# Masked copy of the transposed probabilities moved from VectorE to GpSimd, and the order of the attention units on TensorE

## The chip, the cores and the metric

The kernel runs on one core of a Trainium2 chip. The metric is device time in microseconds (us), the median of three runs. All times below are microseconds unless marked ns.

## What is computed

One decoder layer over 1024 tokens of width 1024. One input projection feeds two token mixers: a gated linear recurrence with four heads, and a sliding-window attention with eight query heads, two key/value heads of 64 columns, a window of 128 and a learned sink for each head. Their outputs go through one output projection into the residual stream, and a gated feed-forward layer follows. The attention part of the reference, cut to what matters:

```python
qb = q.reshape(B, nb, BLOCK, ATTN_KV_HEADS, ATTN_GROUP, ATTN_HD)     # blocks of 128 queries, 256 keys: previous, current
scores = jnp.einsum('bnqhgd,bnkhd->bnhgqk', qb, kb)
mask = (rel >= 0) & (rel < WINDOW) & (kpos >= 0)
scores = jnp.where(mask, scores, NEG_INF)
m = jnp.maximum(jnp.max(scores, axis=-1, keepdims=True), s)
p = jnp.exp(scores - m)
denom = jnp.sum(p, axis=-1, keepdims=True) + jnp.exp(s - m)
out = jnp.einsum('bnhgqk,bnkhd->bnqhgd', p / denom, vb)
```

## The kernel before, in words

Each engine is programmed by its own block, and the blocks for TensorE (PE), VectorE (DVE), ScalarE (ACT), GpSimd (POOL) and SyncE (SP) all walk through one list, `order`, that `schedule()` writes. An engine does the steps that concern it in the order of that list and waits on semaphores for the others. Nothing is reordered at run time, so the place of a step in the list is its place in the queue of every engine that takes part in it.

Attention stands in the list as 16 units (2 for each of the 8 blocks of 128 tokens; a unit i is four heads of block i // 2). Since a window of 128 over blocks of 128 means that each query sees exactly 128 keys, the scores of the previous and the current block are merged into one 128 x 128 square for each head (`sc`, three buffers). The steps of a unit:

- `SC`: PE computes the scores (12 matmuls on 64-row tiles of the array, L1511 to L1515); DVE copies the previous block's scores (L1871), lays the current block's over them by a predicate (L1874) and takes the row maximum (L1880). The next unit's `SC` on PE waits for L1874.
- `SE`: ACT takes the exponentials, four instructions with their sums (L1009).
- `SN`: DVE takes the reciprocal of the sums (L1885); POOL multiplies the probabilities by it (L759) and writes a small sink column (L706).
- `TR`: PE transposes the four squares into bank 5 or 6 of PSUM (L1525). DVE multiplies them by the triangular mask `band` into `pT[:, 1]` (L1892), the part that belongs to the current block. ACT copies them in full into `pT[:, 0]` (L1017), from unit 2 on (the first block has no previous one).
- `PV`: PE multiplies values by the transposed probabilities (L1541, on 64-column tiles). The masked part meets `vstep`, the step from the previous block's values to the current one's, and the full part meets the previous block's values, so that both together are the banded product. After each second unit ACT evacuates the result into `att` (L1023).

`pT` is one buffer: `TR` of the next unit writes it only when `PV` has read it. The steps of different units are interleaved by

```python
    for i in range(units + LAG + 1):
        steps.append([s for s in (("PV", i - LAG - 1), ("TR", i - LAG), ("SN", i - 2), ("SC", i), ("SE", i - 1))
                      if 0 <= s[1] < units])
```

with LAG = 3, and `mix` puts them between the parts of the dense projections (`P`: two k-tiles in three products each, 6 matmuls of 512 columns, L1353 to L1355). Each group in `steps` is called a step here. A part P follows the group in all steps but 3, 7 and 11. PE's queue in a step is thus PV(i-4), TR(i-3), SC(i), and then a part P or nothing. In steps 16 to 18 there is no SC any more. The step `WL` (DVE splits off the low half of a projection's weights, L1798), `W` (ACT the high half) and the evacuations of `P` by DVE (L1829) lie between them. After the units, `H1` of the first recurrence head begins: POOL clears `A` and `near`, and ACT computes the sigmoids, from whose results DVE and ACT prepare the head's level products.

Of the kernel before, what the change touches and what calls it, by code (L numbers as in the profile page):

```python
# [5 lines left out]
ALU = mybir.AluOpType  # L6
ACT = mybir.ActivationFunctionType
# [6 lines left out]
P = 128  # L14
# [5 lines left out]
NC = T // P  # L20
HD = 64
AH, KVH = 8, 2
GRP = AH // KVH
# [17 lines left out]
LAG = 3  # L41
# [18 lines left out]
def schedule():  # L60
# [60 lines left out]
    order = [("W", 0), ("WL", 0), ("W", 1), ("WL", 1)]  # L121
# [7 lines left out]
    units = 2 * NC  # L129
    steps = []  # L130
    for i in range(units + LAG + 1):
        steps.append([s for s in (("PV", i - LAG - 1), ("TR", i - LAG), ("SN", i - 2), ("SC", i), ("SE", i - 1))
                      if 0 <= s[1] < units])
    order += mix(take(13), steps[:units], lead=1) + mix(take(4), steps[units:units + LAG])

    order.remove(("WL", 7))
    order.insert(order.index(("PV", 1)), ("WL", 7))

    order += [("H1", 0)]
    steps = [steps[units + LAG], [("HK", 0)], [("HQ", 0)], [("HS", 0), ("H2", 0)], [("HM", 0)], [("HD", 0)],  # L140
             [("LV", 0, 0), ("EB", 0)], [("LX", 0, 0), ("KT", 0)], [("KE", 0), ("LV", 0, 1), ("LV", 0, 2)]]
    order += mix(take(8 + H0_EXTRA), steps)
    for h in range(NH):
        last = h == NH - 1
        steps = []
# [14 lines left out]
        else:  # L160
# [11 lines left out]
            steps = [[("OC", h, c)] for c in range(NC)] + [[("OS", h)]]  # L172
# [49 lines left out]
def build(nc, xT, wv, wproj, wo_a, wo_b, wo_c, wg, wu, wd, gain1, gain2, lbl, ogain, qgain, kgain, sinks, yT):  # L222
    ctx = ExitStack()
    with ctx:
        used = {}

        def at(name, kb, shape, dt=F32):

            return nc.alloc_sbuf_tensor_at(name, shape, dt, offset=16640 + int(kb * KB))
# [10 lines left out]
        band = at("band", 1.5, [P, P])  # L240
# [51 lines left out]
        vstep = at("vstep", 183, [P, NC, P])  # L292
        asq = at("asq", 167, [P, 2, T])
        asqhi, asqlo = at("asqhi", 175, [P, T], F32R), at("asqlo", 179, [P, T], F32R)
        pT = at("pT", 179, [P, 2, GRP * P])
        ars = at("ars", 183, [P, T])

        K = at("K", 147, [P, T])
# [93 lines left out]
        ps = ctx.enter_context(nc.psum_tensor("ps", [P, 8, HALF], F32))  # L392
# [25 lines left out]
        s_tr, s_pte0, s_pte1 = sem("probs_t"), sem("probs_t_prev_evac"), sem("probs_t_cur_evac")  # L418
        s_pv, s_attev = sem("att_out"), sem("att_out_evac")
# [40 lines left out]
        order = schedule()  # L460
# [214 lines left out]
        def _(pool):  # L675
# [29 lines left out]
            def sink_column(i):  # L705
                return nc.gpsimd.tensor_copy(sc[:, i % 3, :, P].rearrange("p (g j) -> p g j", g=KVH),  # L706
                                             sink.rearrange("p (g u j) -> p g u j", g=KVH, u=2)[:, :, i % 2, :])
# [39 lines left out]
            for step in order:  # L747
                if step[0] == "AS" and step[1] < 4:
                    i = step[1]
                    pool.wait_ge(s_pev, 2 * i + 2)  # L750
                    if i >= 2:
                        pool.wait_ge(s_asl, i - 1)
                    nc.gpsimd.tensor_tensor(asq[:, i % 2, :], kq[:, i, :], kq[:, i, :], ALU.mult).then_inc(s_asq, 1)
                elif step[0] == "SN":
                    i = step[1]
                    r = i % 3
                    pool.wait_ge(s_rden, i + 1)
                    probs = sc[:, r, :, 0:P]
                    nc.gpsimd.tensor_tensor(probs, probs, rden[:, 4 * r:4 * r + 4].unsqueeze(2)  # L759
                                            .broadcast_to([P, GRP, P]), ALU.mult).then_inc(s_prob, 1)  # L760
                    if i + 3 < 2 * NC:
                        sink_column(i + 3).then_inc(s_sinkc, 1)
                elif step == ("SC", 0):
                    pool.wait_ge(s_ass, 10)
                    pool.wait_ge(s_const, 16 * N_CONST)
                    for i in range(3):
                        sink_column(i)
                    nc.gpsimd.memset(sc[:, 0:2, :, 0:P], NEG).then_inc(s_setup, 1)
                    pool.wait_ge(s_kqlo, 5)
                    pool.wait_ge(s_vev, 2 * NC)  # L770
                    kv = v[:, :, NH * P:2 * VW]
                    nc.gpsimd.tensor_tensor(vstep[:, 1:NC, :], kv[:, 1:NC, :], kv[:, 0:NC - 1, :], ALU.subtract)\
                        .then_inc(s_vstep, 1)
                elif step[0] == "H1":
                    hh = step[1]
                    if hh == 0:
                        pool.wait_ge(s_tr, 2 * NC)
                        nc.gpsimd.memset(A[:, :], 0.0).then_inc(s_setup, 1)
                        pool.wait_ge(s_pte1, 2 * NC)
                        nc.gpsimd.memset(near[:, :, :], 0.0).then_inc(s_setup, 1)  # L780
                    pool.wait_ge(s_sig, 3 * hh + 3)
                    gv = rawg[hh % 2]
                    nc.gpsimd.tensor_tensor(gv[:, :], gv[:, :], DD[0][:, :], ALU.mult).then_inc(s_gm, 1)
                elif step[0] == "XS":
                    weight_sums(step[1])
                elif step[0] == "NA":
                    x = step[1]
                    for i, (m, m2) in enumerate(NSUM[x]):
                        pool.wait_ge(s_nsq, 8 * x + m2 + 1)
                        if i and (m2 - m > 1 or m == 0):  # L790
                            pool.wait_ge(s_nacc, 7 * x + i)
                        nc.gpsimd.tensor_tensor(nsq[x][m][:, :], nsq[x][m][:, :], nsq[x][m2][:, :], ALU.add)\  # L792
                            .then_inc(s_nacc, 1)
# [85 lines left out]
        def _(act):  # L879
# [81 lines left out]
            for step in order:  # L961
                kind = step[0]
# [19 lines left out]
                elif kind == "AS":  # L982
                    i = step[1]
# [7 lines left out]
                elif kind == "AN":  # L991
                    i = step[1]
# [7 lines left out]
                elif kind == "AH":  # L1000
                    i = step[1]
                    act.wait_ge(s_an, i + 1)
                    nc.scalar.activation(kqhi[:, i, :], kqn[i][:, :], ACT.Copy).then_inc(s_kqhi, 1)
                elif kind == "SE":
                    i = step[1]
# [5 lines left out]
                                             accum_out=den[:, 4 * r + j:4 * r + j + 1]).then_inc(s_exp, 1)  # L1011
                elif kind == "TR":
                    i = step[1]
                    if i >= 2:
                        act.wait_ge(s_pte1, i + 1)
                        act.wait_ge(s_pv, i)
                        nc.scalar.activation(pT[:, 0, :], ps[:, 5 + i % 2, :], ACT.Copy).then_inc(s_pte0, 1)  # L1017
                elif kind == "PV":
                    i = step[1]
                    if i % 2 == 1:  # L1020
                        n = i // 2
# [94 lines left out]
                elif kind == "MS":  # L1116
                    i = step[1]
# [9 lines left out]
                elif kind == "NS":  # L1127
                    x2 = step[1]
                    t = slice(x2 * HALF, (x2 + 1) * HALF)
# [3 lines left out]
                elif kind == "NL":  # L1133
                    x2 = step[1]
                    t = slice(x2 * HALF, (x2 + 1) * HALF)
# [4 lines left out]
                elif kind == "NH":  # L1140
                    x2 = step[1]
                    t = slice(x2 * HALF, (x2 + 1) * HALF)
# [16 lines left out]
                elif kind == "OL":  # L1159
                    i = step[1]  # L1160
# [189 lines left out]
        def _(pe):  # L1350
# [59 lines left out]
            for step in order:  # L1410
                kind = step[0]
                if kind == "V":
                    _, n, t = step
                    g = n * NC + t
# [14 lines left out]
                elif kind == "P":  # L1429
                    _, g, part = step  # L1430
# [5 lines left out]
                    for k in (part, part + 4) if u == N_PROJ - 1 else (2 * part, 2 * part + 1):  # L1436
                        w = slice(k * P, (k + 1) * P)
                        t = slice(half * HALF, (half + 1) * HALF)
# [6 lines left out]
                elif kind == "O":  # L1445
                    _, g, part = step
# [13 lines left out]
                    for k in range(2 * part, min(2 * part + 2, n_k)):  # L1460
                        t = slice(half * HALF, (half + 1) * HALF)
# [22 lines left out]
                elif kind == "AM":  # L1484
                    i = step[1]
# [6 lines left out]
                    for half in range(2):  # L1492
                        t = slice(half * HALF, (half + 1) * HALF)
# [3 lines left out]
                elif kind == "SC":  # L1497
                    i = step[1]
# [18 lines left out]
                elif kind == "TR":  # L1517
                    i = step[1]
                    pe.wait_ge(s_prob, i + 1)
                    if i >= 2:  # L1520
                        pe.wait_ge(s_pte1, i - 1)
                    if i >= 4:
                        pe.wait_ge(s_pte0, i - 3)
                    for j in range(GRP):
                        mm = nc.tensor.transpose(ps[:, 5 + i % 2, j * P:(j + 1) * P], sc[:, i % 3, j, 0:P], ident[:, :])  # L1525
                    mm.then_inc(s_tr, 1)
                elif kind == "PV":
                    i = step[1]
# [5 lines left out]
                        pe.wait_ge(s_vstep, 1)  # L1534
                    for t in (1, 0) if n else (1,):
                        if t == 0:
                            pe.wait_ge(s_pte0, i - 1)
                        for g in range(KVH):
                            vals = (vstep[:, n, HD * g:HD * g + HD] if n and t else
                                    v[:, max(n - 1, 0), NH * P + HD * g:NH * P + HD * g + HD])  # L1540
                            mm = nc.tensor.matmul(ps[HD * g:HD * g + HD, 7, pair * 2 * P:(pair + 1) * 2 * P], vals,  # L1541
                                                  pT[:, t, g * 2 * P:(g + 1) * 2 * P],
                                                  start=(t == 1), stop=(t == 0 or n == 0))
                    mm.then_inc(s_pv, 1)
                elif kind == "KT":
# [174 lines left out]
        def _(dve):  # L1720
# [71 lines left out]
            for step in order:  # L1792
# [88 lines left out]
                elif kind == "SN":  # L1881
# [2 lines left out]
                    dve.wait_ge(s_exp, 4 * (i + 1))  # L1884
                    nc.vector.reciprocal(rden[:, q4], den[:, q4]).then_inc(s_rden, 1)  # L1885
                    dve.wait_ge(s_rden, i + 1)
                elif kind == "TR":
                    i = step[1]
                    dve.wait_ge(s_tr, i + 1)
                    if i:  # L1890
                        dve.wait_ge(s_pv, i)
                    nc.vector.tensor_tensor(pT[:, 1, :].rearrange("p (j q) -> p j q", q=P),  # L1892
                                            ps[:, 5 + i % 2, :].rearrange("p (j q) -> p j q", q=P),
                                            band[:, :].unsqueeze(1).broadcast_to([P, GRP, P]), ALU.mult).then_inc(s_pte1, 1)
                elif kind == "HK":
                    hh = step[1]
                    dve.wait_ge(s_sig, 3 * hh + 1)
# [404 lines left out]
```

## Time and profile before

| | |
|---|---|
| time, median of 3 runs | 1094.47 (1093.45 to 1095.52) |
| the profiled execution's own time | 1093.2 |
| its span, first to last instruction | 1091.2 |
| PE busy | 1078.7 (99%) |
| DVE busy | 664.4 (61%) |
| ACT busy | 508.4 (47%) |
| POOL busy | 375.6 (34%) |
| granted TensorE clock | 1.00 |

The span is that of the instructions; 2.0 lie outside of it. Matmuls are pipelined, and each is drawn with a modelled end that overlaps the next one, so PE's time is best read from start to start. PEld is the weight load of TensorE, which overlaps the matmuls. The attention units lie between 136 and 202 of the span. A group of a timeline gives the start, the duration, the engine, the line, the operation, the tiles with their shapes, and how many instructions are merged.

### The profile page before, as it was taken

The page shows a single profiled execution, that of the slowest core. Times are in us where ns is not written, and L with a number is a line of the kernel's source. Part 1 is how long each engine was busy: PE and PEld are TensorE (multiplying, and loading weights), DVE is VectorE, ACT ScalarE, POOL GpSimd, SP SyncE. Part 2 cuts the span into 40 slices and gives each one's busy share as a digit, 9 for nine tenths or more (in the row PEclk, how much of TensorE's full clock was granted, in tenths as well). Part 3 has the DMA queues.
Part 4 walks back from the last instruction along what each step waited for, and adds up shares of the span by engine and source line. Part 5 has one row for each costly group of instructions (what it writes and reads, how often), then busy time and mean ns, then how long its engine had stood idle before and what let it go on. Part 6 is the DMA issues. An engine that isn't in the chain of part 4 may idle for free.

```text
span 1091.2 us, 16138 instructions
## 1 busy us (share of the span) xinstructions
PE 1078.7 (99%) x6322; PEld 881.4 (81%) x6322; DVE 664.4 (61%) x814; ACT 508.4 (47%) x807; POOL 375.6 (34%) x337
## 2 busy tenths in 40 slices
PE   9999999999999999989999999999999999999998
PEld 9998866778878787867888888888888877888886
DVE  7314588578698957995243433334343688777776
ACT  8414456656576635553333333333333554545531
POOL 0301133200000007226536444553645742534462
PEclk9999999999999999999999999999999999999999
DMA  8101100011105133113313313331332784455433
GB/s 290 40 1 58 39 20 21 20 41 41 40 26 188 31 108 153 40 38 128 129 53 126 126 59 126 112 129 49 126 126 67 269 311 159 140 157 162 127 104 155
DMA packets 37387, 112.73 MB, mean 103 GB/s; under 512 B 4929, under 2 KB 9793, under 8 KB 35905
## 3 DMA queue, kind: packets, MB, share of 16 engines
q1 hardware_dynamic: 36880, 111.38, 29.6%
q8 instruction: 51, 0.84, 0.3%
q10 hardware_dynamic: 432, 0.33, 0.1%
q14 instruction: 24, 0.19, 0.1%
HBM read 83.12 MB, written 28.57 MB: 102 GB/s over the span
## 4 chain that ended last, share of the span: by engine, by line
PE 90%; DVE 5%; issue 2%; POOL 2%; ACT 1%; DVEq 0%; POOLq 0%; ACTq 0%
PE ps L1353 28%; PE ps L1355 27%; PE ps L1354 27%; PE ps L1568 1%; PE ps L1541 1%; POOL nsq L792 1%; DVE olo L1760 1%; PE ps L1525 1%; PE ps L1583 1%; PE ps L1585 1%; DVE h L1755 1%; PE ps L1511 1%; PE ps L1588 1%; PE ps L1594 1%; PE ps L1392 0%
## 5 line engine op out<-in xcount | busy, mean ns | idle before, releaser
L1727 DVE TENSOR_TENSOR glo<-graw,ghi 128x1024 fp32r<-128x1024 f32 x21 | 26.2, 1246 | 147.5 <-POOL s34raw L696 147.3
L1353 PE MATMUL ps<-uhi,whi 128*128 128x512 f32 x272 | 112.3, 413 | 0.0
L1355 PE MATMUL ps<-uhi,wlo 128*128 128x512 f32 x272 | 106.4, 391 | 0.0
L1354 PE MATMUL ps<-ulo,whi 128*128 128x512 f32 x272 | 106.3, 391 | 0.0
L2103 DVE TENSOR_TENSOR yacc<-ps,yacc 128x512 f32<-128x512 f32 x104 | 68.5, 683 | 10.7 <-PE ps L1355 10.5
L1353 PE MATMUL ps<-ubhi,arhi 128*128 128x512 f32 x176 | 69.3, 394 | 0.9 <-DVE arlo L2078 0.5
L1353 PE MATMUL ps<-ohi,s12hi 128*128 128x512 f32 x168 | 65.6, 391 | 3.1 <-DVE olo L1760 2.5
L1354 PE MATMUL ps<-ublo,arhi 128*128 128x512 f32 x176 | 68.6, 390 | 0.0
L1355 PE MATMUL ps<-ubhi,arlo 128*128 128x512 f32 x176 | 68.6, 390 | 0.0
L1353 PE MATMUL ps<-ohi,s34hi 128*128 128x512 f32 x168 | 65.5, 390 | 0.8 <-ACT ps L1187 0.8
L1354 PE MATMUL ps<-olo,s12hi 128*128 128x512 f32 x168 | 65.5, 390 | 0.0
L1353 PE MATMUL ps<-u2hi,ghi 128*128 128x512 f32 x168 | 65.4, 390 | 0.0
L1354 PE MATMUL ps<-u2lo,ghi 128*128 128x512 f32 x168 | 65.4, 390 | 0.0
L1355 PE MATMUL ps<-ohi,s12lo 128*128 128x512 f32 x168 | 65.4, 390 | 0.0
L1354 PE MATMUL ps<-olo,s34hi 128*128 128x512 f32 x168 | 65.4, 390 | 0.0
L1355 PE MATMUL ps<-ohi,s34lo 128*128 128x512 f32 x168 | 65.4, 390 | 0.0
L1355 PE MATMUL ps<-u2hi,glo 128*128 128x512 f32 x168 | 65.4, 389 | 0.0
L805 POOL TENSOR_TENSOR hst<-sg,up 128x512 f32<-128x512 f32 x21 | 29.5, 1403 | 102.7 <-issue 60.7
L689 POOL TENSOR_TENSOR s12raw<-uraw 128x512 f32<-128x512 f32 x21 | 28.9, 1374 | 103.8 <-DVE rec L2010 68.5
L2071 DVE TENSOR_TENSOR ublo<-ubraw,ubhi 128x1024 fp32r<-128x1024 f32 (+1 forms) x44 | 50.2, 1151 | 18.4 <-ACT ubhi L1221 18.3
L1353 PEld LDWEIGHTS ps<-uhi,whi 128*128 128x128 f32 x272 | 51.1, 188 | 12.2 <-issue 0.9
L1355 PEld LDWEIGHTS ps<-uhi,wlo 128*128 128x128 f32 x272 | 51.1, 188 | 11.2
(335 smaller groups left out, 2942.7 us busy)
## 6 DMA issues: line engine op xcount, KB each, us to landing
hidden<-hst SPq DMA_DIRECT2D x11, 1792.0 KB, 6.0
ubraw<-hidden SPq DMA_DIRECT2D x33, 512.0 KB, 5.3
graw<-wg SPq DMA_DIRECT2D x21, 512.0 KB, 4.3
uraw<-wu SPq DMA_DIRECT2D x21, 512.0 KB, 3.5
wraw<-wproj SPq DMA_DIRECT2D x17, 512.0 KB, 3.5
araw<-wd SPq DMA_DIRECT2D x22, 384.0 KB, 4.7
h<-xT SPq DMA_DIRECT2D x8, 512.0 KB, 4.8
h_kept<-h SPq DMA_DIRECT2D x16, 256.0 KB, 2.0
```

The source lines that it names most:

```text
L689: nc.gpsimd.tensor_tensor(sw[:, 0:HALF], uw[:, 0:HALF], uw[:, HALF:D], ALU.add).then_inc(s_sum, 1)
L792: nc.gpsimd.tensor_tensor(nsq[x][m][:, :], nsq[x][m][:, :], nsq[x][m2][:, :], ALU.add)\
L805: nc.gpsimd.tensor_tensor(hst[:, 4 if g % 2 else 7, :], sg2[:, :], upg[:, :], ALU.mult)\
L1353: nc.tensor.matmul(out, whi_, xhi_, start=first, stop=False, skip_group_check=seeded)
L1354: nc.tensor.matmul(out, whi_, xlo_, start=False, stop=False, skip_group_check=seeded)
L1355: return nc.tensor.matmul(out, wlo_, xhi_, start=False, stop=last, skip_group_check=seeded)
L1511: nc.tensor.matmul(out, kqhi[r, hq, qs], kqhi[r, 0, ks], start=True, stop=False)
L1525: mm = nc.tensor.transpose(ps[:, 5 + i % 2, j * P:(j + 1) * P], sc[:, i % 3, j, 0:P], ident[:, :])
L1541: mm = nc.tensor.matmul(ps[HD * g:HD * g + HD, 7, pair * 2 * P:(pair + 1) * 2 * P], vals, pT[:, t, g * 2 * P:(g + 1) * 2 * P], start=(t == ...
L1727: nc.vector.tensor_tensor((glo2 if g == 2 else glo[g % 2])[:, :], graw[g % 2][:, :], ghi[g % 2][:, :].bitcast(F32), ALU.subtract).then_inc ...
L2071: nc.vector.tensor_tensor(ublo[j % 3][i][:, :, :], ubraw[j % 3][i][:, :, :], ubhi[j % 3][i][:, :, :].bitcast(F32), ALU.subtract).then_inc( ...
L2103: nc.vector.tensor_tensor(yacc[q][:, t, :], ps[:, bank, :], yacc[q][:, t, :], ALU.add).then_inc(s_dadd, 1)
```

## The change

Five edits that belong together. The order of the steps becomes SN(i-2), AE(i-4), TR(i-3), PV(i-4), SC(i), SE(i-1), where `AE` is a new name for ACT's evacuation into `att`, which stood under `PV` before. `pT` becomes two buffers of two parts each, the second at an address that the later tile `A` uses. ACT copies the transposed probabilities in full for all 16 units (14 before). DVE's masked product is gone; POOL makes it from ACT's copy in SBUF. The waits follow: PE's transposes wait for ACT's copy of two units before, PV waits for POOL's product and ACT's copy, and the clearing of `A` waits for the last PV.

```diff
-        steps.append([s for s in (("PV", i - LAG - 1), ("TR", i - LAG), ("SN", i - 2), ("SC", i), ("SE", i - 1))
-                      if 0 <= s[1] < units])
+        steps.append([s for s in (("SN", i - 2), ("AE", i - LAG - 1), ("TR", i - LAG), ("PV", i - LAG - 1), ("SC", i),
+                                  ("SE", i - 1)) if 0 <= s[1] < units])
...
-    order.insert(order.index(("PV", 1)), ("WL", 7))
+    order.insert(order.index(("TR", 2)), ("WL", 7))
...
-        pT = at("pT", 179, [P, 2, GRP * P])
+        pT = [at(f"pT{i}", kb, [P, 2, GRP * P]) for i, kb in enumerate((179, 175))]
...
+                elif step[0] == "TR":
+                    i = step[1]
+                    pool.wait_ge(s_pte0, i + 1)
+                    if i >= 2:
+                        pool.wait_ge(s_pv, i - 1)
+                    nc.gpsimd.tensor_tensor(pT[i % 2][:, 1, :].rearrange("p (j q) -> p j q", q=P),
+                                            pT[i % 2][:, 0, :].rearrange("p (j q) -> p j q", q=P),
+                                            band[:, :].unsqueeze(1).broadcast_to([P, GRP, P]), ALU.mult).then_inc(s_pte1, 1)
...
-                        pool.wait_ge(s_tr, 2 * NC)
+                        pool.wait_ge(s_pv, 2 * NC)
                         nc.gpsimd.memset(A[:, :], 0.0).then_inc(s_setup, 1)
...
                 elif kind == "TR":
                     i = step[1]
+                    act.wait_ge(s_tr, i + 1)
                     if i >= 2:
-                        act.wait_ge(s_pte1, i + 1)
-                        act.wait_ge(s_pv, i)
-                        nc.scalar.activation(pT[:, 0, :], ps[:, 5 + i % 2, :], ACT.Copy).then_inc(s_pte0, 1)
-                elif kind == "PV":
+                        act.wait_ge(s_pv, i - 1)
+                    nc.scalar.activation(pT[i % 2][:, 0, :], ps[:, 5 + i % 2, :], ACT.Copy).then_inc(s_pte0, 1)
+                elif kind == "AE":
...
                     if i >= 2:
-                        pe.wait_ge(s_pte1, i - 1)
-                    if i >= 4:
-                        pe.wait_ge(s_pte0, i - 3)
+                        pe.wait_ge(s_pte0, i - 1)
...
                         if t == 0:
-                            pe.wait_ge(s_pte0, i - 1)
+                            pe.wait_ge(s_pte0, i + 1)
...
-                elif kind == "TR":
-                    i = step[1]
-                    dve.wait_ge(s_tr, i + 1)
-                    if i:
-                        dve.wait_ge(s_pv, i)
-                    nc.vector.tensor_tensor(pT[:, 1, :].rearrange("p (j q) -> p j q", q=P),
-                                            ps[:, 5 + i % 2, :].rearrange("p (j q) -> p j q", q=P),
-                                            band[:, :].unsqueeze(1).broadcast_to([P, GRP, P]), ALU.mult).then_inc(s_pte1, 1)
```

## Rows read from the trace of the kernel before

**Rows 1.** The page, busy time, share and instructions of PE.

```profile
PE 1078.7 (99%) x6322; PEld 881.4 (81%) x6322; DVE 664.4 (61%) x814; ACT 508.4 (47%) x807; POOL 375.6 (34%) x337
```

**Rows 2.** Busy time of each engine in a stretch of the units.

```profile
166.00:174.00 8.00, 8.00 (x62) 5.23 (x60) 6.20 (x12) 5.70 (x20) 2.35 (x4) 1.00 0.01 3
```

**Rows 3.** Waits from 142 to 200: who for whom, total, times, longest.

```profile
ACT pT L1017 <- DVE pT L1892: 16.8, 14, 2.4
...
PE ps L1525 <- POOL sc L759: 0.6, 1, 0.6
```

**Rows 4.** Timeline of PE: a step with a part P, and the next.

```profile
153.95 0.66 PE L1525 MATMUL ps<-ident,sc 128*128 128x128 f32 x4
154.54 0.39 PE L1511 MATMUL ps<-kqhi 64*128 64x256 f32 x2
...
155.45 0.50 PE L1353 MATMUL ps<-uhi,whi 128*128 128x512 f32 x1
...
157.03 0.65 PE L1541 MATMUL ps<-pT,vstep 128*64 128x256 f32 x4
157.52 0.60 PE L1541 MATMUL ps<-pT,v 128*64 128x256 f32 x4
158.05 0.66 PE L1525 MATMUL ps<-ident,sc 128*128 128x128 f32 x4
158.63 0.39 PE L1511 MATMUL ps<-kqhi 64*128 64x256 f32 x2
...
161.28 0.39 PE L1511 MATMUL ps<-kqhi 64*128 64x256 f32 x2
```

**Rows 5.** Timeline of PE, early units: transposes behind a part P, later scores.

```profile
143.25 0.40 PE L1355 MATMUL ps<-uhi,wlo 128*128 128x512 f32 x1
143.49 0.60 PE L1525 MATMUL ps<-ident,sc 128*128 128x128 f32 x4
144.02 0.39 PE L1511 MATMUL ps<-kqhi 64*128 64x256 f32 x2
...
146.78 0.39 PE L1511 MATMUL ps<-kqhi 64*128 64x256 f32 x2
```

**Rows 6.** Timeline of PE, late units: transposes ahead of a part P.

```profile
192.04 0.66 PE L1525 MATMUL ps<-ident,sc 128*128 128x128 f32 x4
192.45 0.47 PE L1353 MATMUL ps<-uhi,whi 128*128 128x512 f32 x1
```

**Rows 7.** Timeline of DVE in step 2 and the beginning of step 3.

```profile
142.15 0.69 DVE L1871 COPY sc<-ps 128x512 f32<-128x512 f32 x1 [1.00 <-PE ps L1515]
...
143.65 0.69 DVE L1880 TENSOR_REDUCE smax<-sc 128x4 f32<-128x516 f32 x1
144.26 0.68 DVE L1892 TENSOR_TENSOR pT<-ps,band 128x512 f32<-128x512 f32 x1
144.85 0.17 DVE L1885 RECIPROCAL smax<-smax 128x4 f32<-128x4 f32 x1
```

**Rows 8.** Timeline of ACT: a full copy, the exponential behind it, an evacuation.

```profile
152.56 0.60 ACT L1017 ACTIVATE pT<-ps 128x512 f32<-128x512 f32 x1 [1.99 <-DVE pT L1892]
153.05 0.40 ACT L1009 ACTIVATE sc<-sc,smax 128x129 f32<-128x129 f32 x1
...
158.16 0.60 ACT L1023 ACTIVATE att<-ps 128x512 f32<-128x512 f32 x1 [0.57 <-PE ps L1541]
```

**Rows 9.** Timeline of POOL: SN of unit 1 and its sink column.

```profile
145.10 1.04 POOL L759 TENSOR_TENSOR sc<-sc,smax 128x512 f32<-128x512 f32 x1 [2.70 <-DVE smax L1885]
146.09 0.19 POOL L706 COPY sc<-small 128x4 f32<-128x4 f32 x1
```

**Rows 10.** POOL's groups of instructions over the span, shapes apart: busy, mean ns.

```profile
L805 POOL TENSOR_TENSOR hst<-sg,up 128x512 f32<-128x512 f32 x21 | 29.5, 1403 | 102.7 <-issue 60.7 <-ACT sg L1207 42.0
...
L816 POOL TENSOR_TENSOR hst<-hst 128x512 f32<-128x512 f32 x11 | 20.1, 1823 | 37.4 <-DVE hst L2049 37.4
...
L783 POOL TENSOR_TENSOR rawg<-rawg,D 128x1024 f32<-128x1024 f32 x4 | 10.0, 2508 | 135.7 <-ACT D L1035 135.7
```

More of the change, by code:

```diff
@@ L1541, in _ @@
                             mm = nc.tensor.matmul(ps[HD * g:HD * g + HD, 7, pair * 2 * P:(pair + 1) * 2 * P], vals,
-                                                  pT[:, t, g * 2 * P:(g + 1) * 2 * P],
+                                                  pT[i % 2][:, t, g * 2 * P:(g + 1) * 2 * P],
                                                   start=(t == 1), stop=(t == 0 or n == 0))
```

## The prediction

> **What bounds the kernel now.** I read the page first: PE is busy for 99% of the span [rows 1], so the end moves only with what PE's queue gains or loses. Next I read the table of stretches over the units: in eight microseconds PE has no gap, DVE works 6.20, ACT 5.70 and POOL 2.35, at full clock [rows 2]. DVE's share is large, but relieving it is worth nothing while PE is not waiting. The view of waits says that PE hardly waits for anybody here: the one wait that opens a gap in its matmuls is 0.6 for POOL's SN of unit 1; the 16.8 that ACT waits for DVE's masked product cost PE nothing [rows 3]. So two questions are left for PE's timeline: what the new order costs or saves between kinds of matmuls, and whether the new, longer way to a finished `pT` is late anywhere.
>
> **The order on PE.** Read from start to start [rows 4]: TR 0.59, SC 0.91, P 1.58, PV 0.49 + 0.53 = 1.02, together 4.10. A step without P takes 158.63 to 161.28 = 2.65. The last of the six matmuls of a part P is followed by another 128-row matmul after 0.23 or 0.24, while PV comes later. Transposes directly behind P pay nothing for the change-over (143.25 to 143.49 = 0.24) and take 0.53 up to SC, against 0.58 behind PV [rows 4, 5]. A part P is 0.34 for its first and 5 x 0.23 for the others, 1.48, when nothing of another tile shape follows; so 0.10 of the 1.58 are the change-over to PV. The new step is P 1.48 + TR 0.53 + PV 1.02 + SC 0.91 = 3.94, that is 0.16 less. The trace has no TR in front of PV and no PV in front of SC. I bound them by the exits it has: TR to P is 0.41 [rows 6] and TR to SC 0.53 to 0.59, PV to TR 0.53. I take the dearer exit for TR, since the tile shape changes as it does towards SC, and 0.53 for PV; at the cheap end a step would gain 0.12 more, and if PV to SC cost a further 0.06 it would gain 0.10 instead of 0.16.
>
> Such steps end at SC5 (one pair of matmuls in PV1), SC6, SC7, SC9 to SC11 and SC13 to SC15: 9 x -0.16 = -1.4. The three steps without P keep three changes of shape out of three: 0.91 + 0.58 + 1.02 = 2.51 against 2.65, so -0.3 for steps 7 and 11 (step 3 is worked out below). In the last steps (TR13 to TR15, no SC) the old order had TR to P at 0.41; the new one pays 0.53 for TR to PV and saves the 0.10 after P: +0.03 each, +0.1 in all.
>
> **The price of POOL's product.** It has two full 128x512 streams of f32 in SBUF. Below lies SN, 1.04, whose second operand is four columns wide [rows 9]. Half of the 1024-column product `rawg` x `D` is 1.25, and `sg` x `up` at the very shape has a mean of 1.40 [rows 10]. I take 1.25, since those two have two real streams and the attention stretch shows SN undisturbed at 1.04; the ends are 1.04 and 1.40, with 1.82 (L816) for a disturbed one. The Trainium skill, GPSIMD Engine Reference, Elementwise, side-by-side cycle accounting, puts a two-input product at about 2.6 cycles per element and VectorE near twice as fast, so it speaks against this move; by it alone the product would be some 1.1 plus dispatch, an estimate from that page, and the sum below about 0.6 lower. The trace agrees on the ratio (1.25 by the rows for POOL against 0.68 on DVE).
>
> **Where it is late.** ACT's copy for unit j comes in step j+3, POOL's product behind it, PV(j) in step j+4. In front of the copy now stands AE, in each step with odd i-4, and AE waits for PV(i-4), which PE does after TR(i-3). Call the start of TR 0: PV starts at 0.53, AE 1.13 after it (157.03 to 158.16 [rows 4, 8]), 1.66; the copy 0.49 later, 2.15, ready at 2.75; POOL's product from 2.80 to 4.05, PV(j) can start at 4.10. PE is there at 3.94 + 0.53 = 4.47 after a step with P: 0.4 to spare. After a step without P it is there at 0.53 + 1.02 + 0.91 + 0.58 = 3.04: it waits 1.05. Behind the waiting PV stand SC and the next P, so the wait is lost. This holds for steps 7 and 11, whose AE3 and AE7 are odd: PV4 and PV8, 2.1 in all. In step 17 (AE13, no SC) PE comes at 1.48 + 0.53 + 1.02 + 0.53 = 3.56, against 4.10: PV14 waits 0.5.
>
> The other way to be late is POOL's queue: the product of unit j stands behind SN(j+1), which waits for the reciprocal, which stands behind DVE's block of SC(j+2). That block is 142.15 to 144.26 = 2.11 [rows 7]. From the end of SC(j+2) on PE: 0.1 + 2.11 + 0.25 + 0.99 + 0.19 + 1.25 + 0.05 = 4.9. PE gets to PV(j) after 1.48 + 0.53 + 1.02 + 0.91 + 1.48 + 0.53 = 5.95, so 1.0 is to spare, less 0.6 where DVE also evacuates a projection; with WL8 (1.13) in front, PV11 waits 0.1. In the beginning it bites: without DVE's product the reciprocal of unit 1 runs at 144.26 instead of 144.85, SN1 from 144.51, its sink column until 145.68, the product of unit 0 until 146.93, PV0 at 146.98 with 0.55, SC4 at 147.53 instead of 146.78 [rows 5, 7, 9]: +0.75, with the old wait of 0.6 already inside.
>
> What DVE and SP get: 16 x 0.6 of DVE is freed and hidden, since PE has no wait for it; no DMA moves. ACT gets two copies more (0.6 each) in steps 3 and 4, beside free time. POOL clears `A` after PV15 instead of TR15, but has nothing else to do before the sigmoids. If that cover were gone, the gate product `rawg` would be late, and it is used only at the head's end.
>
> **Sum.** SC4 +0.75, nine steps -1.4, two short steps -0.3, last steps +0.1, PV4 and PV8 +2.1, PV14 +0.5, PV11 +0.1: **+1.9**. From 1093.2 (span 1091.2 and 2.0 around it) that gives 1095.1; the profiled execution is 1.3 under the median, so I predict 1096.4. Later stages shift as they are, since they are bound by PE too.
>
> **The rivals.** A change under 0.2% (2.2) cannot be told from none in this kernel.
> 1. *The product is hidden, only the order counts.* If copy and product are ready in time everywhere, -1.4, -0.3 and +0.1 stand, and SC4 is where it was, since TR1 still waits for SN1 (145.61 + 0.58 + 0.55 = 146.74): -1.6, 1092.9. For it: DVE's and ACT's earlier slots; against it: AE ahead of the copy, by the program's own queue. With the cheap exit of TR (12 x 0.12) it would reach -3.0, 1091.5. Chance 0.17, of which 0.08 beyond 0.2%.
> 2. *POOL becomes the bound (slower).* If the product takes over 1.32, the four or five late places pass +2.2. Place: PV0, PV4, PV8, PV11, PV14; each 0.1 more costs 0.45. At 1.40 it gives +2.6, 1097.1; at 1.82, where PV2, PV3, PV7 and PV12 run out of their slack as well, some +5.5, 1100. For it: L805 at 1.40 and L816 at 1.82; against it: SN is an undisturbed 1.04. Chance 0.28.
> 3. *The gain of the order is not there.* If TR to PV and PV to SC cost as much as what they replace, the -1.4 goes: +3.3, 1097.8. Against it: rows 5, where P to TR costs nothing. Chance 0.07.
>
> The forecast itself has 0.48, with its own range of 1095.1 to 1097.6 (product 1.04 to 1.40 at five places, -0.9 to +0.7, and 0.05 at twelve changes of shape). The likelier part of it, 0.46, lies within 0.2%. **Chances:** faster 0.08; same 0.46 + 0.09 = 0.55; slower 0.28 + 0.07 + 0.02 = 0.37. **Range:** from rival 1 to past the 1.40 end of rival 2 and rival 3, 1092.5 to 1098.8, which leaves out the cheap exits and the disturbed product.
>
> **What the profile after would show.** PE: TR 0.24 behind the last matmul of P, steps with P at 3.94 from SC to SC; a PE wait for POOL's product before PV0, PV4 and PV8 (about 1 each for the last two) and PV14; ACT: AE3 and AE7 ahead of the copies, with waits for PE; POOL: 16 new products of 1.25; DVE: no L1892, waits for PE in its place. I am wrong if the product is far from 1.25, if PV behind TR costs more than 1.1, or if PE's wait before SC for L1874 grows.

## The result, and the profile after

The changed kernel takes 1096.78 (median of 17 runs, 1095.69 to 1098.64) against 1093.68 (17 runs, 1092.72 to 1095.52): a ratio of 1.0031, 95% interval 1.0025 to 1.0037: slower by 3.1 by the medians and by 3.4 (2.7 to 4.0) by the ratio. The forecast was +1.9 and 1096.4. The time lies in the range, but the change is larger than the forecast one and over the 0.2% that the prediction took as the least to be told; its likeliest outcome was "same" (0.55), and "slower" had 0.37.

The page of the changed kernel, and the waits of PE and POOL from 140 to 208 (who for whom, total, times, longest):

```profile
span 1094.0 us, 16142 instructions
...
PE 1077.4 (98%) x6322; PEld 882.3 (81%) x6322; DVE 656.6 (60%) x798; ACT 509.2 (47%) x809; POOL 397.3 (36%) x353
```

```profile
POOL pT L768 <- ACT pT L1025: 4.6, 7, 1.5
...
PE ps L1547 <- POOL pT L768: 3.6, 4, 1.1
...
PE ps L1547 <- issue: 0.7, 1, 0.7
PE ps L1531 <- POOL sc L759: 0.6, 1, 0.6
```

DVE gave up 7.8 of busy time and POOL took 21.7, of which 20.6 are the 16 products and 1.0 is one SN that took longer (below). What counts is the second fence. Before, PE had a gap of 0.6 in this stretch [rows 3]; now POOL's masked product (L768) opens four in front of PV (L1547), 3.6 in all, and a fifth of 0.7 has no releaser. The columns are gaps between drawn matmuls, whose modelled ends overlap; the waits below are taken from start to start and are somewhat longer.

The timeline of PE in the changed kernel, steps 6 to 8 (the counterpart of [rows 4]):

```profile
155.98 0.39 PE L1519 MATMUL ps<-kqhi 64*128 64x256 f32 x2
...
158.15 0.39 PE L1363 MATMUL ps<-uhi,wlo 128*128 128x512 f32 x1
158.38 0.60 PE L1531 MATMUL ps<-ident,sc 128*128 128x128 f32 x4
158.91 0.65 PE L1547 MATMUL ps<-pT,vstep 128*64 128x256 f32 x4
159.40 0.60 PE L1547 MATMUL ps<-pT,v 128*64 128x256 f32 x4
159.93 0.39 PE L1519 MATMUL ps<-kqhi 64*128 64x256 f32 x2
...
160.84 0.66 PE L1531 MATMUL ps<-ident,sc 128*128 128x128 f32 x4
162.62 0.65 PE L1547 MATMUL ps<-pT,vstep 128*64 128x256 f32 x4 [1.13 <-POOL pT L768]
```

A step with a part P takes 159.93 - 155.98 = 3.95 from SC to SC, where it took 4.10: the transposes follow P after 0.23, TR to PV is 0.53, PV to SC 0.53. Then comes step 8, behind a step without P: TR5 at 160.84, and PV4 not at 161.42 but at 162.62, a wait of 1.20. What it waited for, on ACT and POOL in the same kernel:

```profile
160.04 0.60 ACT L1031 ACTIVATE att<-ps 128x512 f32<-128x512 f32 x1 [3.64 <-PE ps L1547]
160.54 0.59 ACT L1025 ACTIVATE pT<-ps 128x512 f32<-128x512 f32 x1
```

```profile
159.41 1.04 POOL L759 TENSOR_TENSOR sc<-sc,smax 128x512 f32<-128x512 f32 x1 [2.13 <-DVE smax L1891]
160.40 0.19 POOL L706 COPY sc<-small 128x4 f32<-128x4 f32 x1
161.21 1.27 POOL L768 TENSOR_TENSOR pT<-pT,band 128x512 f32<-128x512 f32 x1 [0.62 <-ACT pT L1025]
```

AE3 starts 1.66 after TR4 (158.38), when PV3 is done, and holds the copy until 160.54, 2.16 after TR4; with nothing in front of it the copy starts 0.63 after TR4 (experiment 2), so it is 1.5 late. POOL, done with SN5 and its sink column, waits 0.62 for the copy; its product ends at 162.48. PV8 has the same picture at 178.17 and the same 1.2.

One thing was not foreseen. DVE and POOL of the changed kernel, step 5:

```profile
151.18 0.17 DVE L1891 RECIPROCAL smax<-smax 128x4 f32<-128x4 f32 x1
151.38 1.23 DVE L1804 TENSOR_TENSOR wlo<-wraw,whi 128x1024 fp32r<-128x1024 f32 x1
152.52 0.68 DVE L1877 COPY sc<-ps 128x512 f32<-128x512 f32 x1
```

```profile
151.43 2.08 POOL L759 TENSOR_TENSOR sc<-sc,smax 128x512 f32<-128x512 f32 x1 [1.71 <-DVE smax L1891]
153.45 0.18 POOL L706 COPY sc<-small 128x4 f32<-128x4 f32 x1
153.60 1.27 POOL L768 TENSOR_TENSOR pT<-pT,band 128x512 f32<-128x512 f32 x1
154.88 1.04 POOL L759 TENSOR_TENSOR sc<-sc,smax 128x512 f32<-128x512 f32 x1
```

SN3 takes 2.08 where all others take 1.04. It began 0.05 after WL7 (L1804) on DVE. Two steps of PE pay for it:

```profile
153.07 0.39 PE L1363 MATMUL ps<-uhi,wlo 128*128 128x512 f32 x1
153.56 0.66 PE L1531 MATMUL ps<-ident,sc 128*128 128x128 f32 x4
154.97 0.65 PE L1547 MATMUL ps<-pT,vstep 128*64 128x256 f32 x4 [0.75 <-issue]
```

TR3 comes 0.26 late (153.07 + 0.23 = 153.30), for SN3, and PV2 0.83 late (153.56 + 0.58 = 154.14), for the product queued behind it (153.60 + 1.27 = 154.87): this is the gap for which the profile names no releaser. Together 1.1.

To compare kernels without what lies ahead of and behind the units, I take on PE the time from the start of SC2 to that of the first level product of head 0: 84.22 before (141.07 to 225.29), 87.88 after (140.91 to 228.79), +3.66. It is called the stretch from here on. Each stretch is read from one profiled execution.

### The profile page after: what moved, and what is told of

It reads as the page before. It is cut to its first block, busy times and chain, and to the rows that moved or that the text cites. A ratio compares the mean times of both kernels' runs of the same rounds, so it can differ in the third digit from the quotient of the medians.

```text
span 1094.0 us, 16142 instructions
## 1 busy us (share of the span) xinstructions
PE 1077.4 (98%) x6322; PEld 882.3 (81%) x6322; DVE 656.6 (60%) x798; ACT 509.2 (47%) x809; POOL 397.3 (36%) x353
## 4 chain that ended last, share of the span: by engine, by line
PE 87%; DVE 5%; issue 3%; POOL 3%; ACT 1%; DMA 1%; SPq 0%; DVEq 0%; POOLq 0%; ACTq 0%
PE ps L1361 27%; PE ps L1363 26%; PE ps L1362 26%; PE ps L1574 1%; PE ps L1547 1%; POOL pT L768 1%; DMA araw<-wd 1%; DVE olo L1766 1%; POOL sc L759 1%; PE ps L1591 1%; PE ps L1589 1%; DVE h L1761 1%; PE ps L1594 1%; PE ps L1600 1%; PE ps L1400 0%
```

## The experiments

All ratios are against runs of the kernel before on the same chip.

| kernel | stretch | against before | ratio, 95% interval |
|---|---|---|---|
| before | 84.22 | | |
| changed | 87.88 | +3.66 | 1.0031 (1.0025 to 1.0037) |
| 1: WL7 moved | 87.16 | +2.94 | 1.0026 (1.0017 to 1.0036) |
| 2: evacuation behind the copy | 85.91 | +1.69 | 1.0013 (1.0005 to 1.0022) |
| 3: product on DVE, new order | 83.41 | -0.81 | 0.9991 (0.9983 to 1.0000) |
| 4: product on POOL, old order | 89.11 | +4.89 | 1.0043 (1.0031 to 1.0056) |
| 5: edits of 1 and 2 | 85.10 | +0.88 | 1.0004 (0.9994 to 1.0013) |
| 6: 3 with WL7 moved | 82.81 | -1.41 | 0.9986 (0.9977 to 0.9995) |
| 7: WL8 beside SN11 | 87.92 | +3.70 | one run, 1096.32 |
| 8: product on DVE, old order | 84.22 | 0.00 | 0.9995 (0.9986 to 1.0004) |

**1. WL7 moved.**

```diff
-    order.insert(order.index(("TR", 2)), ("WL", 7))
+    order.insert(order.index(("SN", 7)), ("WL", 7))
```

> The changed kernel with one edit: DVE's split of the weights WL7 stands in front of SN7's reciprocal instead of behind SN3's. Theory: SN3 on POOL took 2.08 instead of 1.04 because WL7 (two SBUF inputs) ran beside it on DVE, and that made TR3 wait 0.3 and PV2 wait 0.8. Then SN3 is 1.04 here, both waits are gone, and the kernel is 1.0 to 1.2 us faster than the changed one (about 1095.7, or +2.0 against the kernel before). Rival: SN3 is long for another reason (its place in POOL's queue), and PV2's wait comes from POOL's own queue; then the time stays at +3.1 and SN3 at 2.08.

POOL in step 5 of this kernel:

```profile
151.30 1.04 POOL L759 TENSOR_TENSOR sc<-sc,smax 128x512 f32<-128x512 f32 x1 [1.70 <-DVE smax L1891]
152.28 0.19 POOL L706 COPY sc<-small 128x4 f32<-128x4 f32 x1
152.43 1.29 POOL L768 TENSOR_TENSOR pT<-pT,band 128x512 f32<-128x512 f32 x1
```

SN3 is back at 1.04, TR3 is in time, and at SC6 the kernel is 1.0 ahead of the changed one. It gives 0.26 back in step 10, where PV6 waits for a product behind an SN7 that WL7 now delays, so the stretch is 0.72 shorter, against an expected 1.0 to 1.2. In whole times the gain, 0.5 by the ratios, is not told from zero (the intervals overlap); the trace shows it.

**2. Evacuation behind the copy.**

```diff
-        (("SN", i - 2), ("AE", i - LAG - 1), ("TR", i - LAG), ("PV", i - LAG - 1), ("SC", i),
+        (("SN", i - 2), ("TR", i - LAG), ("AE", i - LAG - 1), ("PV", i - LAG - 1), ("SC", i),
```

> The changed kernel with one edit: on ACT the evacuation AE stands behind the full copy, not in front of it. Theory: AE waits for the PV that PE does behind the transposes, and holds the copy back by about 1.5 in steps 7, 11 and 17; without it PV4 and PV8 wait about 0.45 instead of 1.2 each, since POOL is then busy with SN5 and SN9 until 2.2 after TR, and PV14 does not wait: 2.1 us faster than the changed kernel, +1.0 against the kernel before. Rival: POOL's product is the bound whatever stands in front of the copy, since its queue holds SN and product back to back; then the waits stay at 1.1 and the time at +3.1.

ACT, POOL and PE of this kernel in steps 7 and 8:

```profile
158.87 0.60 ACT L1025 ACTIVATE pT<-ps 128x512 f32<-128x512 f32 x1 [2.62 <-PE ps L1531]
159.90 0.60 ACT L1031 ACTIVATE att<-ps 128x512 f32<-128x512 f32 x1 [0.43 <-PE ps L1547]
```

```profile
159.28 1.04 POOL L759 TENSOR_TENSOR sc<-sc,smax 128x512 f32<-128x512 f32 x1 [2.13 <-DVE smax L1891]
160.26 0.19 POOL L706 COPY sc<-small 128x4 f32<-128x4 f32 x1
160.41 1.27 POOL L768 TENSOR_TENSOR pT<-pT,band 128x512 f32<-128x512 f32 x1
```

```profile
160.69 0.66 PE L1531 MATMUL ps<-ident,sc 128*128 128x128 f32 x4
161.83 0.65 PE L1547 MATMUL ps<-pT,vstep 128*64 128x256 f32 x4 [0.48 <-POOL pT L768]
```

The copy starts 0.63 after TR4 (158.24) instead of 2.16. The product does not follow it at once: it is now behind SN5 in POOL's queue, as foreseen, and PV4 waits 161.83 - 160.69 - 0.58 = 0.56 instead of 1.20. PV14 does not wait. The stretch is 1.97 shorter than the changed kernel's (2.1 expected): two thirds of the 3.1 that PE lost to late products at PV4, PV8 and PV14 was ACT's queue, not POOL's speed.

**3. Product on DVE, in the new order.** POOL's branch for `TR` is gone; DVE has one again, ACT's copy waits for it, and PE's transposes also wait for `s_pte1`.

```diff
+                elif kind == "TR":
+                    i = step[1]
+                    dve.wait_ge(s_tr, i + 1)
+                    if i >= 2:
+                        dve.wait_ge(s_pv, i - 1)
+                    nc.vector.tensor_tensor(pT[i % 2][:, 1, :].rearrange("p (j q) -> p j q", q=P),
+                                            ps[:, 5 + i % 2, :].rearrange("p (j q) -> p j q", q=P),
...
-                    act.wait_ge(s_tr, i + 1)
+                    act.wait_ge(s_pte1, i + 1)
```

> The changed kernel with the masked product given back to DVE (from PSUM, ahead of ACT's copy, which waits for it as in the kernel before); the new order of the steps and the two buffers of pT stay. Theory: the order alone gains 0.15 in each of some ten steps and costs nothing; the waits of PV0, PV4, PV8 and PV14 were POOL's. Remaining: TR1's wait for SN1 and TR3's wait of 0.3 for an SN3 that still takes 2.08 beside WL7. So -1.3 against the kernel before (-0.8 to -2.0), 4.4 under the changed kernel. Rival 1: the waits come from AE and the order, not from POOL; then it is at +2 or more. Rival 2: DVE, with the product again, now delays L1874 or the reciprocals; then PE waits before SC.

The stretch is 0.81 shorter than before, the ratio 0.9991: every wait for a product is gone, PE waits nowhere before SC, and the steps with P are 3.95. Both rivals of this expectation are out. Of the expected 1.3 a part is lost in step 6: WL7 again starts beside SN3, which takes 2.08, and TR3 waits 0.6 rather than 0.3, since PE arrives earlier.

**4. Product on POOL, in the old order** (with AE behind PV).

```diff
+        (("PV", i - LAG - 1), ("AE", i - LAG - 1), ("TR", i - LAG), ("SN", i - 2), ("SC", i),
...
+    order.insert(order.index(("PV", 1)), ("WL", 7))
```

> The changed kernel with the order of the steps of the kernel before (PV, TR, SN, SC, SE, with AE behind PV); POOL's product and the two buffers stay. Theory: the gain of the order is gone, and PV(i-4) comes 0.6 earlier against TR(i-3), while product i-3 now stands ahead of SN(i-2) on POOL: from the start of a step PV 1.02, copy from 1.71, product 2.35 to 3.6, so PV4 and PV8 wait 1.0, SC4 comes 1.0 later, PV13 and PV14 wait 0.65 each: about +4.3 against the kernel before (+3.0 to +5.0). Rival: the new order is what costs, because AE stands ahead of the copy; then the old order gives +1 or less.

+4.89 in the stretch, 1.0043 in time. PE of this kernel in steps 7 and 8:

```profile
158.30 0.65 PE L1547 MATMUL ps<-pT,vstep 128*64 128x256 f32 x4
158.79 0.60 PE L1547 MATMUL ps<-pT,v 128*64 128x256 f32 x4
159.32 0.66 PE L1531 MATMUL ps<-ident,sc 128*128 128x128 f32 x4
...
162.10 0.65 PE L1547 MATMUL ps<-pT,vstep 128*64 128x256 f32 x4 [1.22 <-POOL pT L768]
```

PV4 waits 1.22, as long as in the changed kernel, although PV3 is done before TR4 here and the evacuation holds nothing back: PE is ready for PV4 at 162.10 - 1.22 = 160.88, only 1.56 after TR4, where the new order leaves 3.04 (158.38 to 161.42). So the new order did not cost; it is 1.2 better (4.89 - 3.66) for the same engines. One thing more stands in this trace: the product of unit 2 (152.44) took 1.67 where the others take 1.27 to 1.29; its first 0.51 ran beside WL7 (151.73 to 152.95). No PV waited for it.

**5. Edits of 1 and 2 together.**

> The changed kernel with both edits of the first and second experiment (WL7 in front of SN7's reciprocal, evacuation behind the copy). Theory: the two causes are separate and add up: 0.7 and 2.0 by the traces, so 2.7 under the changed kernel, +0.4 to +0.6 against the kernel before. Rival: once the copies are early, POOL's own queue is what PV waits for in more steps, and only one of the two gains shows: +1.0 or more.

The stretch is 2.78 shorter than the changed kernel's, against 0.72 + 1.97 = 2.69: the two causes add up, and the time is that of the kernel before. What remains of POOL's product is the late start of PV0, 0.55 each at PV4 and PV8 and about 0.2 each at PV6 and PV11; the order's gain pays for most of it.

**6. Experiment 3 with WL7 moved.**

> The third experiment's kernel (product on DVE from PSUM, new order, two buffers) with WL7 in front of SN7's reciprocal. Theory: SN3 falls from 2.08 to 1.04, TR3 no longer waits (0.6), so 0.5 to 0.6 faster than the third experiment: -1.3 to -1.6 against the kernel before, ratio about 0.9987. Rival: DVE, which has the product again, is late in step 9 with WL7 in front, and the gain is lost there: ratio as in the third experiment, 0.9991.

0.60 shorter than experiment 3, as expected, 1.41 shorter than before, 0.9986: faster than the kernel before by 1.5 and than the changed one by 4.9, by the ratios. The one wait of PE left in the units is TR1's 0.6 for SN1.

**7. WL8 beside SN11**, in the changed kernel.

```diff
+    order.remove(("WL", 8))
+    order.insert(order.index(("TR", 10)), ("WL", 8))
```

> The changed kernel with WL8 put directly behind SN11's reciprocal, as WL7 stands behind SN3's (it stood in front of SN12's, with POOL idle). Theory: DVE's difference of two SBUF tiles holds POOL back for nearly its whole length, so SN11 takes 2.08 and SN3 still 2.08, all others 1.04; the end moves by less than 0.3, since PV11's wait of 0.2 goes and PV10 waits 0.1. Rival: SN3 was long for a reason of its own (DMA, first use); then SN11 stays at 1.04.

DVE and POOL of this kernel in step 13 (two lines are added above, so L761 and L1806 are the L759 and L1804 of the changed kernel):

```profile
182.61 0.17 DVE L1893 RECIPROCAL smax<-smax 128x4 f32<-128x4 f32 x1
182.81 1.23 DVE L1806 TENSOR_TENSOR wlo<-wraw,whi 128x1024 fp32r<-128x1024 f32 x1
```

```profile
182.86 2.08 POOL L761 TENSOR_TENSOR sc<-sc,smax 128x512 f32<-128x512 f32 x1 [1.31 <-DVE smax L1893]
184.89 0.19 POOL L708 COPY sc<-small 128x4 f32<-128x4 f32 x1
```

SN11 takes 2.08 as soon as a WL starts 0.05 before it, and nothing else was moved. With experiment 1, which takes WL7 away and gets 1.04, this shows the cause from both sides. The stretch is the same within 0.04.

**8. Product on DVE, in the old order**, with two buffers and sixteen full copies.

> The old order with the product on DVE from PSUM, but with two buffers of pT and full copies for all 16 units: what is left of the change without POOL's product and without the new order. Theory: nothing waits for the second buffer in the kernel before, so the same as before within 0.3 us (ratio 0.9997 to 1.0003), and the third experiment's gain is the order's. Rival: the second buffer is what gained; then it is at -1 us.

The stretch is 84.22, as before to the hundredth: second buffer and additional copies are worth and cost nothing. So the gain of experiment 3 is the order's alone. By the traces, that is: in whole times experiment 3 and 8 are not told apart, and only experiment 6 is clearly under the kernel before.

## Why the prediction was right or wrong, point by point

The forecast was a little slower, likeliest too little to tell, and it came out as clearly slower. The places and causes of PE's waits were right but for one step, below. That the time came within 0.4 (1096.4 against 1096.78) is luck: the base, the median of the three runs then known, was 1094.47, 0.8 above the median of 17, and this made up for most of the 1.2 that the change was short. The same goes for rival 2: the change passed its +2.2, but not because of a slower product. By the terms of the sum, in the stretch:

| term | forecast | measured |
|---|---|---|
| SC4 later (PV0 waits, TR1 waits) | +0.75 | +0.77 |
| nine steps with P | -1.4 | -0.15 each, -1.35 |
| steps 7 and 11 without P, apart from the waits | -0.3 | -0.28 |
| PV4 and PV8 | +2.1 | +2.41 (1.20 and 1.21) |
| PV14 | +0.5 | +0.68 |
| PV11 | +0.1 | +0.17 |
| steps without SC | +0.1 | +0.16 |
| TR3 and PV2, through an SN3 of 2.08 | not in it | +1.09 |
| sum | +1.9 | +3.65 (stretch +3.66) |

- *The order.* Right: P to TR costs nothing (0.23, as between two matmuls of P), both unknown exits were the 0.53 taken, and a step with P, which has one change of tile shape fewer, is 0.15 shorter. The two steps without P keep three changes and are 0.14 shorter all the same, so the number of changes alone does not explain the gain; it also matters which kinds stand next to each other, and why is not shown. Experiments 3, 6 and 8 isolate the order: -0.81 in the stretch, -1.41 once SN3 is undisturbed.
- *POOL's product.* Taken at 1.25, measured at 1.27 to 1.31 in all 16 (median 1.288). The kernel before had this number: L805 has a median of 1.29, and its mean of 1.40 [rows 10] comes from three of 21 that took 1.86 to 2.27. Rival 2's value of 1.32 or more did not occur, nor did POOL become the bound: it waits for ACT's copy in seven of the steps.
- *Where it is late.* Right in place and cause, 0.15 short for each of PV4 and PV8: a signal from ACT to POOL took 0.08 and one from POOL to a PV that waits for it 0.14 (162.48 to 162.62), where 0.05 each stood in the forecast.
- *The step that failed* is the check of POOL's queue, "0.1 + 2.11 + 0.25 + 0.99 + 0.19 + 1.25 + 0.05 = 4.9", in which 0.99 stands for an SN that runs alone. The forecast followed WL8 through DVE's queue but not WL7, which the change puts right behind SN3's reciprocal, so that both start together. The runs showed 2.08 for this SN and +1.09 for PE. In the kernel before no WL overlapped an SN; DVE did WL7, the product and the reciprocal in front of SN3:

```profile
150.71 1.22 DVE L1798 TENSOR_TENSOR wlo<-wraw,whi 128x1024 fp32r<-128x1024 f32 x1
151.84 0.69 DVE L1892 TENSOR_TENSOR pT<-ps,band 128x512 f32<-128x512 f32 x1
152.44 0.17 DVE L1885 RECIPROCAL smax<-smax 128x4 f32<-128x4 f32 x1
```

```profile
152.69 1.04 POOL L759 TENSOR_TENSOR sc<-sc,smax 128x512 f32<-128x512 f32 x1 [3.46 <-DVE smax L1885]
```

  It is the new place of WL7 that does it, not the missing product: in experiment 3 DVE has the product again and SN3 still takes 2.08. The forecast had 1.82 for a disturbed instruction in rival 2, but tied it to the product, not to the one SN beside which a DVE instruction with two SBUF inputs had just been put.
- *What was left open.* The stretch is 3.66 longer, the profiled spans differ by 2.8 and the medians by 3.1. From the first level product to the end of the span the ten profiled kernels take between 864.4 and 866.0, with the same instructions there, so some 0.7 of that difference is later stages that vary; what varies in them is not known.

## What to carry to other kernels

On an engine that bounds the kernel, read from start to start what each kind of instruction costs behind each other kind: regrouping the same instructions was worth 0.15 a step, without any engine working less. Before a producer is moved to an engine with free time, lay out its whole chain (here PE, ACT, POOL, PE) for the shortest step, with what stands ahead of each link in its engine's queue; the idle share of POOL said nothing, and a 0.6 evacuation in front of the copy cost PE two thirds of what the late products at PV4, PV8 and PV14 cost, since it waited for work that PE did later. And when an instruction gets a new place in a queue, look at what now runs at the same time on the other engines, not only at what starts earlier or later.

## What the runs showed of the hardware that was not expected

A POOL instruction and a DVE instruction with two SBUF inputs hardly run at the same time: in the traces here the one that starts later stands nearly still until the other is done, and the one that started first keeps its time. In the units DVE was first: SN takes 2.08 instead of 1.04 when it starts 0.05 after the 128x1024 difference WL, which keeps its 1.23 (SN3 in the changed kernel and in experiments 2, 3 and 7, SN11 in experiment 7). The kernel before already had such pairs in a later stage, in both directions. Here DVE is first by 0.05 (L1743 takes 0.69), and POOL's L816 takes 1.79, where L819 with the same tiles has a mean of 1.30:

```profile
516.26 0.69 DVE L1743 TENSOR_TENSOR a22lo<-uraw,a22hi 128x512 fp32r<-128x512 f32 x1
516.31 1.79 POOL L816 TENSOR_TENSOR hst<-hst 128x512 f32<-128x512 f32 x1 [2.84 <-DVE hst L2049]
```

And here POOL is first by 0.33: L805 keeps its 1.29, and DVE's L1738, which took 1.22 at its shortest, takes 2.05:

```profile
529.96 1.29 POOL L805 TENSOR_TENSOR hst<-sg,up 128x512 f32<-128x512 f32 x1 [6.74 <-issue]
530.29 2.05 DVE L1738 TENSOR_TENSOR s34lo<-s34raw,s34hi 128x1024 fp32r<-128x1024 f32 x1 [0.46 <-ACT s34hi L941]
```

Beside DVE instructions with an input in PSUM, and in experiment 4 also beside the row maximum with its one input in SBUF (L1886, 0.5 of overlap), SN stayed at 1.03 to 1.05. The Trainium skill, GPSIMD Engine Reference, Specifications, names this contention on the shared SBUF interface with DVE instructions of two SBUF inputs; the trace agrees and adds its size, 1.04 lost for 1.23 of such an instruction.

The profile names no releaser for a wait that ended 0.1 after a POOL instruction (PV2, 154.97), though the four others before a PV are put down to POOL. Experiment 1, which makes the product earlier, takes this gap away: a gap marked "issue" was here a wait like the others.
